# Hybrid encoder step on one Trainium2 core: 32 instead of 16 tokens of the second group gathered row by row, their dots ahead of the second phase, and low halves on GpSimd that wait for one-hots on VectorE

## The reference, cut to what matters

```python
def peer_block(tok, wq, keys, u, v):
    ...
    s = jnp.einsum('phcd,hckd->phck', qr, keys)          # 2 x 128 sub-keys per head
    top_s, top_i = lax.top_k(s, PEER_TOPK)               # 16 of each
    cand = top_s[:, :, 0, :, None] + top_s[:, :, 1, None, :]
    best, j = lax.top_k(cand.reshape(...), PEER_TOPK)    # 16 experts per head
    ...
    g = jax.nn.softmax(best, axis=-1)
    act = jax.nn.gelu(jnp.einsum('phkd,pd->phk', u[eidx], tok))
    return jnp.einsum('phk,phkd->pd', (g * act), v[eidx])
```

## Time and profile before

| | |
|---|---|
| median of 3 runs | 1956.92 us (1955.56 to 1957.82) |
| span of the profiled execution | 1955.2 us |
| TensorE busy in it | 1926.3 us (99%) |
| VectorE | 1491.8 us (76%) |
| ScalarE | 865.3 us (44%) |
| GpSimd | 885.0 us (45%) |
| moved by DMA | 469.37 MB, mean 240 GB/s |

### The profile page before, as it was taken

The page is one execution under the profiler, slowest core; times in us unless marked ns, Lnnn a source line. Parts: engine busy times, 40 slices in busy tenths (PEclk is TensorE's granted clock), DMA queues, the critical chain, the costliest instruction groups (busy, mean ns, idle before and its releaser), DMA issues.

```text
span 1955.2 us, 34516 instructions
## 1 busy us (share of the span) xinstructions
PE 1926.3 (99%) x12628; PEld 1215.0 (62%) x12628; DVE 1491.8 (76%) x2955; ACT 865.3 (44%) x1315; POOL 885.0 (45%) x558
## 2 busy tenths in 40 slices
PE   9999999999999999999999999999999999999997
PEld 7647777777777776555556666655555555555554
DVE  7975566555365668999899999951899888899885
ACT  6444446655443333333356666653333333333331
POOL 3732222221333454676877767775344442344320
PEclk9999999999999999999999999999999999999998
DMA  5622113223342223776989999986999999899971
GB/s 201 226 95 98 46 60 123 91 85 132 121 158 87 95 69 116 235 280 248 355 281 364 372 364 370 363 279 233 361 398 400 387 357 347 337 393 385 372 270 49
DMA packets 161051, 469.37 MB, mean 240 GB/s; under 512 B 17368, under 2 KB 59360, under 8 KB 160424
## 3 DMA queue, kind: packets, MB, share of 16 engines
q1 hardware_dynamic: 81824, 240.98, 33.7%
q0 software_dynamic: 41728, 151.03, 21.0%
q10 hardware_dynamic: 37384, 75.84, 10.5%
HBM read 402.98 MB, written 64.80 MB: 239 GB/s over the span
## 4 chain that ended last, share of the span: by engine, by line
PE 79%; DVE 15%; issue 2%; POOL 2%; ACT 1%; DMA 1%; ACTq 0%; DVEq 0%; POOLq 0%; SPq 0%
PE ps L2311 28%; PE ps L1854 27%; PE ps L1973 10%; PE ps L1870 3%; DVE rows L1640 2%; PE ps L2127 1%; POOL w_lo L588 1%; PE ps L2251 1%; PE ps L2252 1%; DVE eq L1627 1%; DVE eq L1625 1%; PE ps L2330 1%; DVE hot L1706 1%; PE ps L2107 1%; PE ps L2185 1%
## 5 line engine op out<-in xcount | busy, mean ns | idle before, releaser
L588 POOL TENSOR_TENSOR w_lo<-raw,w_hi 128x1024 bf16<-128x1024 f32 x229 | 508.5, 2225 | 642.7 <-ACT w_hi L698 619.8
L698 ACT ACTIVATE w_hi<-raw 128x1024 bf16<-128x1024 f32 x357 | 374.5, 1051 | 364.4 <-PE ps L2311 190.3
L1854 PE MATMUL ps<-act_hi,w_hi 128*128 128x432 bf16 (+1 forms) x1040 | 358.2, 346 | 0.7 <-DVE proj L1205 0.7
L1854 PE MATMUL ps<-act_lo,w_hi 128*128 128x432 bf16 (+1 forms) x1040 | 358.3, 346 | 0.0
L1854 PE MATMUL ps<-act_hi,w_lo 128*128 128x432 bf16 (+1 forms) x1040 | 358.3, 346 | 0.0
L2311 PE MATMUL ps<-W_hi,w_hi 128*128 128x432 bf16 x992 | 343.4, 346 | 0.8 <-issue 0.8
L2311 PE MATMUL ps<-W_hi,w_lo 128*128 128x432 bf16 x992 | 343.4, 346 | 0.0
L2311 PE MATMUL ps<-W_lo,w_hi 128*128 128x432 bf16 x992 | 343.4, 346 | 0.0
L621 POOL DMA_INDIRECT rows<-in_v_units,rowi x128 | 168.9, 1320 | 314.5 <-DVE accS L1751 296.4
L1058 ACT ACTIVATE hb<-ps 128x432 f32<-128x432 f32 x128 | 68.0, 531 | 310.0 <-PE ps L1854 306.2
L1726 DVE TENSOR_TENSOR w_lo<-raw,w_hi 128x1024 bf16<-128x1024 f32 x124 | 151.5, 1221 | 52.5 <-ACT w_hi L698 52.3
(11 more groups left out here) (454 smaller groups left out, 3396.5 us busy)
## 6 DMA issues: line engine op xcount, KB each, us to landing
raw<-in_u_units SPq DMA_DIRECT2D x128, 512.0 KB, 4.9
raw<-in_v_units SPq DMA_DIRECT2D x128, 512.0 KB, 10.0
raw<-in_units SPq DMA_DIRECT2D x99, 512.0 KB, 3.2
hd<-hb ACTq DMA_DIRECT2D x128, 224.0 KB, 5.5
Hb<-hd SPq DMA_DIRECT2D x32, 896.0 KB, 8.2
gd<-gsb ACTq DMA_DIRECT2D x48, 448.0 KB, 6.9
Gb<-gd SPq DMA_DIRECT2D x32, 672.0 KB, 6.5
gz<-stage ACTq DMA_DIRECT2D x24, 288.0 KB, 2.1
```

Source lines behind the costliest of these rows:

```text
L588: pool.tensor_tensor(w_lo[:, k % RING, :], raw[:, k % RAW, :], w_hi[:, k % RING, :], ALU.subtract).then_inc(lo_ready, 1)
L698: act.activation(w_hi[:, k % RING, :], raw[:, k % RAW, :], ACT.Copy).then_inc(hi_ready, 1)
L1854: last = pe.matmul(ps[:, bank + half, 0:n], w[:, slot, col:col + P], x(k)[:, half * n:(half + 1) * n], start=(k == 0 and w is w_hi and x i ...
```

## The change

- `NX` is 32: 160 tokens are gathered, the dense passes have `TDX` = 416 columns, and there are 52 one-hot steps instead of 54. A second-group gather still has 128 pairs, so there are 32 `x_dot` and 32 `x_combine`.
- The u rows of the second group are fetched by GpSimd in the u half, three behind each low half from chunk 113 on (`X_FETCH`), two at chunk 123. VectorE makes all 32 `x_dot` after its last dot, ahead of the first `gated` of the v half. The `x_combine` stand at every third chunk from 8 on.
- In chunks 49 to 111 GpSimd's low half waits besides for `b_hot`: for chunk c, whose product is that of step s, until VectorE has finished the one-hots of step s+2 (`hots_at`).
- The rows of the last dots are fetched at chunks 108 and 109 instead of up to 114.
- ScalarE's and VectorE's halves of the gated values have 416 columns instead of 448. `xtab` and `sel` lie on tiles no longer used.

```diff
@@ -87,7 +87,7 @@
 NST = TOPK * NPH
-NX = 16
+NX = 32
 TDX = TD - NX
@@ -116,35 +116,31 @@
 LOADS_X = 100
-X_DOT, X_GELU, X_COMB = 4, 64, 72
+X_FETCH, X_COMB, X_STEP = 113, 8, 3
 FIRST_W = {6: (0,), 7: (1, 2, 3)}
...
 DOTS_TWO = 3
+HOTS_AHEAD = 2
 N_SPLIT = 8
...
-def extras_before(c, first):
-    return min(max((c - first + 1) // 2, 0), NX)
 def n_main(c):
-    return c + extras_before(c, X_DOT) + extras_before(c, X_COMB)
+    return NX + c + min(max((c - X_COMB + X_STEP - 1) // X_STEP, 0), NX)
...
-    return n_main(X_DOT + 2 * i) + 1
+    return i
...
-    return n_main(X_COMB + 2 * i) + 1
+    return n_main(X_COMB + X_STEP * i) + 1
@@ -236,7 +232,13 @@
         return J_G * BODY + 2 + d * 2 * BODY // (DOTS_TWO * G_BODY)
-    return J_END * BODY + 2 + (d - during) // 2
+    return J_END * BODY - 4 + (d - during) // 2
+def hots_at(c):
+    body, k = divmod(c - J_G * BODY, BODY)
+    return body * G_BODY + k + HOTS_AHEAD if c > J_G * BODY else 0
@@ -622,9 +626,15 @@
+            def fetch_v(n, table, index):
+                fetch(NST + n, table, (comb_done, n - RG + 1) if n >= RG else (dot_done, NST + n - RG + 1), index)
             v_rows = a["v_units"].rearrange("c e d -> (c e) d")
...
                 if c + RING < NCH:
+                    if 0 < hots_at(c) <= N_STEP:
+                        pool.wait_ge(b_hot, hots_at(c))
                     low_half(U_PEER + RING + c, U_PEER + RING + c)
@@ -637,19 +647,15 @@
                     pool.dma_start(xin[to:to + NX, :, :], xpair[at:at + NX, :, g * NX:(g + 1) * NX]).then_inc(x_moved, 16)
-            def fetch_v(n, table, index):
-                fetch(NST + n, table, (comb_done, n - RG + 1) if n >= RG else (dot_done, NST + n - RG + 1), index)
-            for c in range(NCH):
-                fetch_v(n_main(c), v_rows, rowi[:, c:c + 1])
-                i = (c - X_DOT) // 2
-                if c == X_DOT + 2 * i and 0 <= i < NX:
+                for i in [i for i in range(NX) if min(X_FETCH + i // 3, NCH - 1) == c]:
                     if i == 0:
...
                     fetch_v(n_dot(i), a["u_rows"], rowx[:, i:i + 1])
-                i = (c - X_COMB) // 2
-                if c == X_COMB + 2 * i and 0 <= i < NX:
+            for c in range(NCH):
+                fetch_v(n_main(c), v_rows, rowi[:, c:c + 1])
+                i = (c - X_COMB) // X_STEP
+                if c == X_COMB + X_STEP * i and 0 <= i < NX:
                     fetch_v(n_comb(i), v_rows, rowx[:, i:i + 1])
@@ -1116,7 +1122,7 @@
                 act.wait_ge(w_mul, c + 1)
-                act.activation(W_hi[:, slot, :], wb[:, slot % 2, :], ACT.Copy).then_inc(w_hi_done, 1)
+                act.activation(W_hi[:, slot, 0:TDX], wb[:, slot % 2, 0:TDX], ACT.Copy).then_inc(w_hi_done, 1)
@@ -1136,11 +1142,9 @@
-            with act.Fori(1, X_GELU // RING) as i:
-                v_body(i)
-            act.wait_ge(comb_done, n_dot(NX - 1) + 1)
+            act.wait_ge(comb_done, NX)
             act.activation(xtab[:, 1, :], xtab[:, 0, :], ACT.Gelu_apprx_tanh).then_inc(x_acts, 1)
-            with act.Fori(X_GELU // RING, NCH // RING) as i:
+            with act.Fori(1, NCH // RING) as i:
                 v_body(i)
@@ -1726,13 +1730,10 @@
+            dve.wait_ge(x_moved, 2 * N_XG * 16)
+            dve.tensor_copy(rowx[:, :], xin[:, 0, :]).then_inc(rowx_known, 1)
             for s in range(dots_until(N_STEP), NST):
                 dot(s)
-            dve.wait_ge(b_prod, N_STEP)
-            dve.wait_ge(x_moved, 2 * N_XG * 16)
-            dve.tensor_copy(rowx[:, :], xin[:, 0, :]).then_inc(rowx_known, 1)
@@ -1758,6 +1759,7 @@
                     dve.wait_ge(x_kept, 2)
+                    dve.wait_ge(dot_done, NST)
                 dve.tensor_tensor_reduce(out=row, in0=row, in1=x_rep[:, :], scale=1.0, scalar=0.0, op0=ALU.mult, op1=ALU.add,
@@ -1775,7 +1777,7 @@
                 dve.wait_ge(w_hi_done, c + 1)
-                dve.tensor_tensor(W_lo[:, c % RING, :], wb[:, c % 2, :], W_hi[:, c % RING, :],
+                dve.tensor_tensor(W_lo[:, c % RING, 0:TDX], wb[:, c % 2, 0:TDX], W_hi[:, c % RING, 0:TDX],
                                   ALU.subtract).then_inc(w_lo_done, 1)
@@ -1791,6 +1793,9 @@
+            for s in range(NX):
+                x_dot(s)
+            dve.wait_ge(b_prod, N_STEP)
             for c in range(NCH + LAG):
@@ -1802,11 +1807,8 @@
                 combine(s)
-                i = (s - X_DOT) // 2
-                if s == X_DOT + 2 * i and 0 <= i < NX:
-                    x_dot(i)
-                i = (s - X_COMB) // 2
-                if s == X_COMB + 2 * i and 0 <= i < NX:
+                i = (s - X_COMB) // X_STEP
+                if s == X_COMB + X_STEP * i and 0 <= i < NX:
                     x_combine(i)
...
```

More of the change, by code:

```diff
@@ L290, in program @@
         maskneg = sb("maskneg", [P, P], BF16)
+        iota_at = used[0]
         iota = sb("iota", [P, P], F32)
@@ L295, in program @@
         rx = sb("rx", [P, 2, NTT], F32)
+        tails_at = used[0]
         tails = sb("tails", [P, 2, KT, 3], F32)
@@ L415, in program @@
         rowx = sb("rowx", [P, XHALF], U32)
-        xtab = sb("xtab", [P, 3, XHALF], F32)
-        sel = sb("sel", [P, NX], F32)
+        xtab = place("xtab", iota_at, [P, 3, XHALF], F32)
+        sel = place("sel", tails_at, [P, NX], F32)
         assert used[0] <= nc.sbuf_usable_end, used[0] - nc.sbuf_usable_end
```

## The result

| | before | after |
|---|---|---|
| median | 1957.24 us (1955.56 to 1957.82, 4 runs) | 1991.31 us (1990.6 to 1994.01, 4 runs) |
| span of the profiled execution | 1955.2 us | 1992.3 us |

The change makes the kernel slower: ratio 1.0179, 95% interval 1.0166 to 1.0192. The forecast was 1967 us with a range of 1943 to 1987, so the result lies outside it.

What follows compares the result with a forecast made beforehand. TensorE was taken to bound the kernel through the number and width of matmuls, other engines near their limits. Terms -7 + 25 - 2.6 + 15.5 - 20.5 = +10.4 gave span 1965.6, with 1.7 for the median about 1967 us, range 1943 to 1987.

Steps and rivals of the forecast that it cites:

- the loop: One-hot stage: low half waits for one-hots, row fetch for low half, dot for row, next one-hots for dot: 5.9 + L.
- Up to the first steps, -7: Start of the one-hot stage: two low halves wait, giving 4.4 us at the third product, 7 by the eighth.
- The one-hot stage, +25: Six bodies of 46.0 us, each 4.55 longer, add 27.3 us; the last steps and chunks give back 2.
- L: Time from a row's fetch to its landing in the one-hot stage, taken as 6.5 us.
- rival 1: One-hot stage: rows land early, L 5.0-5.8, stage between -8 and +11, time 1933 to 1953 us; chance 0.22.
- Rival 3: One-hot stage: rows land as late as now, L 7.1 to 7.5, stage +38 to +46, 1980 to 1990; chance 0.13.
- Rival 2: One-hot stage: the row is always there first, L under 5.0, bodies 40.1 us, time 1929 us; chance 0.03.
- Chunks 112 to 127, -2.6: End of the u half: 16 chunks each 0.16 us shorter; low halves there wait for nothing new.
- The extra dots, +15.5: Between the halves: GpSimd's three fetches per low half make TensorE stand 14.7 us, where before it had 0.8.
- The v half, -20.5: 128 v chunks each 0.16 us shorter, at 4.22 us, with VectorE, DMA and halves keeping up.
- rival 5: The v half becomes bound by DMA, chunks 4.4 us over 93 chunks, +17 on the forecast, 1984 us; chance 0.04.
- rival 4: The wait has no bite, low halves pass at once, one-hot stage TensorE-bound, time 1932 us; chance 0.03.

Runs made afterwards that it cites:

- no_wait: The changed kernel without GpSimd's low-half wait for the one-hots: 1950.4 us, ratio 0.9969 to the kernel before.
- x_psum: The changed kernel with the second group's tokens copied to PSUM, so its 32 dots read one operand there: 1986.57 us, ratio 1.0149 to the kernel before.
- wait_alone: The kernel before (432 columns) with nothing but the new wait added: 1998.85 us, ratio 1.0214.
- fetch_early: The changed kernel, wait kept, with the one-hot stage's row fetches two chunks earlier: 1943.34 us, ratio 0.9935 to the kernel before.
- early_no_wait: The changed kernel with row fetches two chunks earlier and no wait for the one-hots: 1991.07 us, ratio 1.0174 to the kernel before.
- lead: The kernel of both, with the second group's fetches from chunk 110 instead of 113, all 32 dots ahead: 1924.29 us, ratio 0.9836 to the kernel before.
- both: The changed kernel with row fetches two chunks earlier and the second group's dots reading tokens from PSUM: 1932.37 us, ratio 0.9878 to the kernel before.

## Why the prediction was wrong

The direction was as forecast, and so were the loop and the queue of GpSimd as what sets the stand. Not forecast was that VectorE and GpSimd stretch each other's operations at the end of the u half. Two places of the sum were priced too low, by 13.0 us (the one-hot stage) and 15.2 us (chunk 112 to the v half). The other two together came out 1.5 us better than forecast (2.3 better and 0.8 worse), which leaves the 26.7 us by which the span missed.

- **Matmul width and TensorE's pace**: right. Bodies without the loop take 40.18 us, v chunks 4.22.
- **Up to the first steps, -7**: -9.3 at chunk 56. The two low halves that wait give 5.5 us (after against no_wait), forecast 4.4. Right in mechanism, a little better than the upper end of 8.
- **The one-hot stage, +25**: +38.0. This is the first step that failed, and the failure is the choice of L. The loop's formula, seven half-turns of 5.9 + L and 2.5 us of second rows, gives 48.0 for a body with L = 7.1. Measured are 48.10 and a median landing of 7.1 (the 31 known ones; 7.0 from fetch to waiting dot, as in x_psum, and 7.1 in wait_alone, with bodies of 48.37 and 48.34). I had taken 6.5 because a body of 46 us would load the DMA engines less. But the landing did not follow the load: 7.1 at 317 GB/s against 7.3 at 365. The 6.2 us of 1290 to 1330 us was no guide to it. In early_no_wait rows land in 6.5 us at 325 GB/s, so such a landing occurs at such a load; why it was 7.1 in the loop stays open. That the fetch leaves together with the next unit's load, which rival 1 had against it, is a candidate that no run varied. Rival 3, rows that land as late as now, was given 0.13 and a stage of +38 to +46, and is what happened there; its time of 1980 to 1990 was passed only because the second step below failed too. The argument against it, "they get 11% more time", is the sentence that was wrong. The clock, for which the sum had nothing here, was at its lower level for 23.9 us of this stage, in five stretches from 1035.3 to 1274.2 us. It has no share in the body as far as the waits tell, since VectorE, through whose steps the loop runs, never waited for TensorE. Rival 2 would have had the rule of the Trainium skill (DMA: Bandwidth & Descriptors, section Anatomy of one DMA - SWDGE path; an estimate of 3.2 us a row) hold under load; the shortest of the 31 known landings was 4.9 us.
- **That the wait can be blamed**: shown from both sides, 43.1 us of span taken out and 43.3 put in. That the late row is the other half of the loop is shown by fetch_early.
- **Chunks 112 to 127, -2.6**: after has 72.6 us from chunk 112 to the last u matmul, before 69.9, forecast 67.3. Up to 1412.17 us ScalarE waits seven times for v units, 29.1 us in all (the last two times for 5.49 and 5.80 us). Their loads wait for late low halves. TensorE waits for ScalarE twice, 2.9 us together, and from 1400.5 us on it has the lower clock for 3.4 us. I had written that the low halves of units 121 to 131 are "late by less than that" and priced it at nothing. The u chunks end 5.3 us later for it. But the first v matmul waited for VectorE's last dots and gates, so in this kernel these 5.3 us only shorten the stand and add nothing to the span: the 15.2 us stand in the table as 5.3 in the u chunks and 9.9 in the stand, and the next point has their cause. In lead, whose stand is 3.0 us, such waits do count.
- **The extra dots, +15.5**: the second step that failed. From the start of chunk 114 (1341.1) to the first v matmul I forecast 73.7 us; it took 88.9. The first turn began where it should (0.6 late). Ten turns took 1412.79 - 1343.3 = 69.5 us instead of 57.5, the last row 9.7 instead of 6.8 until its dot, its issue 0.7 more, dots and gates 1.1 less. The turn was mis-sized because I took the fetch at its bare 0.95 and 1.25 us and the low half at 2.14, and did not ask what VectorE would do beside them. The `x_dot` has two SBUF operands, and the earlier trace rows had shown this very contention for one-hots. x_psum takes it out: its stand is 15.6 us, the forecast 14.7, and from chunk 114 to the first v matmul it takes 1423.8 - 1344.3 = 79.5 us. So contention was 9.4 of the 15.2 us. The other 5.8 remain without it. In x_psum the first turn starts 0.6 us late, ten turns take 1408.05 - 1346.52 = 61.5 us instead of 57.5, because GpSimd waits for row buffers (5.6 us in all before these fetches), and from the last fetch to the first v matmul it is 12.2 us instead of 11.0.
- **The clock, 1.7**: at its lower level for 23.9 us around the stand, 2.2 us lost in the first eight v chunks. About right.
- **The v half, -20.5**: -18.0 with the clock in it, against -18.8. No v chunk waits; rival 5 did not happen. Nor did rival 4: the wait bit 38 times. Rivals 1 and 2 needed landings of 5.8 us or less.

## What to carry to other kernels

When a new wait closes a loop through a DMA, every us of landing counts several times (here 3.5 us of a body), so do not lower the landing because the load will be lighter: here the load fell by 13% and the median by 0.2 us. Cut such a loop at its slackest link: here the fetch two chunks earlier, or the wait one step shorter, was worth 47 to 48 us, and the wait that harmed became useful beside an early fetch. When work is moved beside another engine's work, price both with the stretch that the trace already shows for such pairs, and look first at where the operands lie: an operand moved to PSUM took 9 us out of the stand.

## What was not expected of the hardware

- Row landings do not follow the load alone: the medians are 7.1 us at 317 GB/s (after, single ones up to 11.1), 6.5 at 325 (early_no_wait), 7.3 at 365 (before) and 8.0 at 373 (both).
- An indirect fetch's issue on GpSimd rises from 0.94 to 1.76 us while VectorE works on two SBUF operands, and is 0.94 in the mean when one of them is in PSUM.
- Two engines that share a resource can fall into step: with early fetches and no wait, VectorE's third one-hot took 2.38 us in the mean of 33, and two waits of 1.06 us at the stage's start, with five short ones later, part the run that kept out of it from the one that did not, 45 us apart.
